# Where the selected and the window keys of the requests are transposed: TensorE and PSUM, or VectorE in 32 by 32 blocks

## The reference, cut to what matters

```python
def sample_layer(...):
    past_nsa = gather_pages(c_nsa, page_table)              # [k_cmp, v_cmp, k_slc, v_slc] rows
    kc, vc, cpos, ks, vs, ov = nsa_prepare(concat([past_nsa, nkv[:, :, :4]]), W)
    win_all = concat([win, nkv[:, :, 4:]])
    o_n = nsa_block(nq, qpos, ng, kc, vc, cpos, ks, vs, ov, win_all[:, :, 0], win_all[:, :, 1], wpos, tb)
def nsa_block(...):
    ls = einsum('bthgd,bhtnsd->bhgtns', q, kg) * scale + bias_s     # selected keys
    lw = einsum('bthgd,bshd->bhgts', q, kw) * scale + bias          # window keys
```

## Time and profile before

| | us |
|---|---|
| median of 3 runs | 2698.3 (2696.34 to 2704.59) |
| the profiled execution | 2699.43 |
| its span in the trace | 2697.6 |
| the stage of the requests in it | 807.3 to about 1082.9 |
| TensorE busy over the span | 2592.7 (96%) |

### The profile page before, as it was taken

The page is one execution under the profiler, slowest core; times in us unless marked ns, Lnnn a source line. Parts: engine busy times, 40 slices in busy tenths (PEclk is TensorE's granted clock), DMA queues, the critical chain, the costliest instruction groups (busy, mean ns, idle before and its releaser), DMA issues.

```text
span 2697.6 us, 29317 instructions
## 1 busy us (share of the span) xinstructions
PE 2592.7 (96%) x10863; PEld 1446.0 (54%) x10863; DVE 710.3 (26%) x1959; ACT 532.0 (20%) x1329; POOL 357.5 (13%) x568
## 2 busy tenths in 40 slices
PE   8999998988987999999999999999999999999999
PEld 4554665555555666566665455555555554444443
DVE  0010236665652344101012222222222220101222
ACT  0001025655652333000001121111011110010110
POOL 0000014444443000100001410000000000021110
PEclk9999999998998999999999999999999999999999
DMA  5324530030029776411023101111111115332300
GB/s 177 91 72 116 203 118 1 1 116 1 1 67 240 226 222 207 117 24 47 23 86 66 59 28 37 41 31 31 47 31 31 42 65 189 101 101 102 146 32 31
DMA packets 198599, 227.15 MB, mean 84 GB/s; under 512 B 52191, under 2 KB 149951, under 8 KB 196935
## 3 DMA queue, kind: packets, MB, share of 16 engines
q1 hardware_dynamic: 191674, 199.80, 25.0%
q0 software_dynamic: 5648, 16.33, 1.7%
q10 hardware_dynamic: 1168, 9.58, 1.1%
HBM read 203.60 MB, written 37.99 MB: 90 GB/s over the span
## 4 chain that ended last, share of the span: by engine, by line
PE 60%; ACT 0%; DVE 0%; issue 0%; DVEq 0%
PE ps L2071 24%; PE ps L2121 11%; PE ps L2024 9%; PE ps L2167 5%; PE ps L2017 4%; PE ps L2044 4%; PE ps L2125 1%; PE ps L2006 1%; PE ps L2170 0%; PE ps L2048 0%; PE ps L2078 0%; ACT arena L2257 0%; PE ps L2056 0%; PE ps L2151 0%; DVE arena L2379 0%; DVE qfT L2396 0%
## 5 line engine op out<-in xcount | busy, mean ns | idle before, releaser
L2071 PE MATMUL ps<-xT,qT 128*128 128x480 f32 (+1 forms) x2112 | 648.1, 469 | 0.0
L2071 PEld LDWEIGHTS ps<-xT,qT 128*128 128x128 f32 x2112 | 344.5, 191 | 296.4 <-issue 296.4
L2121 PE MATMUL ps<-arena 128*128 128x512 f32 x704 | 305.3, 593 | 0.0
L2024 PE MATMUL ps<-xT,arena 128*128 128x363 f32 (+1 forms) x768 | 238.1, 467 | 0.0
L2121 PEld LDWEIGHTS ps<-arena 128*128 128x128 f32 x704 | 132.6, 190 | 167.2 <-issue 166.9
L235 PE MATMUL ps<-arena,xT 128*128 128x512 f32 (+1 forms) x512 | 201.6, 552 | 2.9 <-DVE arena L324 1.5
L2024 PEld LDWEIGHTS ps<-xT,arena 128*128 128x128 f32 x768 | 145.4, 189 | 88.8
L929 ACT ACTIVATE arena<-arena 128x640 f32<-128x640 f32 (+15 forms) x256 | 162.8, 638 | 102.2 <-DVE arena L884 57.7
L795 PE MATMUL ps<-ident,arena 128*128 128x128 f32 (+4 forms) x880 | 148.6, 297 | 24.5 <-ACT xT L938 16.0
L983 POOL TENSOR_SCALAR arena<-arena,gates 128x55 f32<-128x55 f32 (+15 forms) x192 | 123.0, 650 | 324.8 <-DVE arena L892 324.6
L2341 DVE TENSOR_SCALAR qfT<-qfT 128x480 f32<-128x480 f32 (+1 forms) x88 | 35.1, 420 | 445.1 <-ACT qfT L2216 445.1
(11 more groups left out here) (299 smaller groups left out, 2465.0 us busy)
## 6 DMA issues: line engine op xcount, KB each, us to landing
arena<-in_w_ffn_down SPq DMA_DIRECT2D x66, 512.0 KB, 3.6
arena<-in_cache_fox_kv SPq DMA_DIRECT2D x72, 256.0 KB, 5.9
xT<-in_cache_fox_kv SPq DMA_DIRECT2D x56, 256.0 KB, 6.7
arena<-in_cache_nsa_kv SPq DMA_DIRECT2D x64, 192.0 KB, 4.7
qT<-in_w_ffn_up SPq DMA_DIRECT2D x22, 512.0 KB, 4.0
qT<-in_w_ffn_gate SPq DMA_DIRECT2D x22, 512.0 KB, 5.3
bias_rows<-rev_dram ACTq DMA_DIRECT2D x8, 1160.0 KB, 19.3
arena<-in_w_in SPq DMA_DIRECT2D x16, 512.0 KB, 5.4
```

What stands on the lines that cost most here:

```text
L2024: mm = pe.matmul(ps[:, 4 * (j % 2) + side, 0:n], at.w_gate[e][:, side, c, :], x[:, c, t0:t0 + n], start=(c == 0), stop=(c == KD - 1))
L2071: mm = pe.matmul(ps[:, 2 * (j % 3) + side, 0:n], at.w_ug[e][:, side, c, :], x[:, c, t0:t0 + n], start=(c == 0), stop=(c == KD - 1))
L2121: mm = pe.matmul(ps[:, q + h, :], hT[:, c, t0:t0 + m], at.w_down[:, load % RING, cols], start=(c == 0), stop=(c == NFF - 1))
```

## The change

The selected and the window keys no longer pass through TensorE and the ring. VectorE transposes them from SBUF to SBUF: one instruction takes a strip of 32 partitions and writes it, block by block of 32 by 32, to 32 other partitions. `selected_turned(r)` has 16 such instructions of 256 elements per partition, `window_turned(r)` 16 of 128, so a round has 32 and 32. They stand behind the copy of `p_fox1` and ahead of `forget_outcome`. `slc_turns`, `win_turns`, six ring entries and their six copies (three on ScalarE, three on VectorE) go. `slc_scores`, `win_scores` and SyncE's `raw_rows` now wait for VectorE's semaphores `slc_turned` and `win_turned`.

```diff
@@ ring_entries @@
-            yield from ((n, f"slc{x}{'ab'[r]}", r) for x in range(2) for r in range(2))
...
-            yield n, "wina", 0
-            yield n, "winb", 1
@@ SyncE @@
             def raw_rows(n):
-                sp.wait_ge(ring_filled, ring.index[n - 1, "slc1b"] + 1)
+                sp.wait_ge(slc_turned, 2 * n)
@@ TensorE @@
-            def slc_turns(n):
-                for x in range(2):
-                    for r in range(2):
-                        b = enter(n, f"slc{x}{'ab'[r]}")
-                        for j in range(4):
-                            mm = turn(b, j * P, P, at.raw[:, r, 2 * x + j // 2, j % 2, 256:384])
-                        mm.then_inc(ring_filled, 1)
-
-            def win_turns(n):
-                pe.wait_ge(win_in, 32 * (n + 1))
-                for r in range(2):
-                    b = enter(n, f"win{'ab'[r]}")
-                    for j in range(4):
-                        mm = turn(b, j * P, P, at.win[:, r, j, 0:P])
-                    mm.then_inc(ring_filled, 1)
...
             def slc_scores(n):
                 if n:
                     pe.wait_ge(nsa_saved, n)
+                pe.wait_ge(slc_turned, 2 * n + 2)
                 for x in range(2):
-                    consumed(n, f"slc{x}a")
-                    consumed(n, f"slc{x}b")
...
             def win_scores(n):
-                consumed(n, "wina")
-                consumed(n, "winb")
+                pe.wait_ge(win_turned, 2 * n + 2)
@@ ScalarE @@
-                    for x in range(2):
-                        save(n, f"slc{x}a", ...)
...
-                    save(n, "wina", at.winT[:, 0, :], ps[:, ring.bank(n, "wina"), :])
@@ VectorE @@
+            def selected_turned(r):
+                for q in range(4):
+                    for z in range(4):
+                        rows = at.raw[z * 32:(z + 1) * 32, r, :, :, 256 + q * 32:256 + (q + 1) * 32]
+                        columns = at.slcT[q * 32:(q + 1) * 32, r, :].rearrange("p (a q t) -> p a t q", a=4, t=2)
+                        ins = nc.vector.transpose(columns[:, :, :, z * 32:(z + 1) * 32], rows)
+                ins.then_inc(slc_turned, 1)
+
+            def window_turned(r):
+                for q in range(4):
+                    for z in range(4):
+                        ins = nc.vector.transpose(at.winT[q * 32:(q + 1) * 32, r, :].rearrange("p (j t) -> p j t", j=4)[:, :, z * 32:(z + 1) * 32],
+                                                  at.win[z * 32:(z + 1) * 32, r, :, q * 32:(q + 1) * 32])
+                ins.then_inc(win_turned, 1)
...
-                    for x in range(2):
-                        save(n, f"slc{x}b", ...)
                     dve.wait_ge(fox_exp, n + 1)
                     inverse(n, fox_inv, at.sums[:, FOX_C:FOX_C + 1], fox_inverse, 2 * n)
                     save(n, "p_fox1", at.pT_fox[:, 4:8, :], tiles(ring.bank(n, "p_fox1"), 4))
+                    dve.wait_ge(raw_in, 256 * (n + 1))
+                    for r in range(2):
+                        selected_turned(r)
+                    dve.wait_ge(win_in, 32 * (n + 1))
+                    for r in range(2):
+                        window_turned(r)
                     if n < N_ - 1:
                         forget_outcome(n)
...
-                    save(n, "winb", at.winT[:, 1, :], ps[:, ring.bank(n, "winb"), :])
```

More of the change, by code:

```diff
@@ L1228, in request_attention @@
      win_exp, imp_ready, imp_saved, pick_step, picked, slc_biased, nsa_coef, nsa_pv, nsa_step, nsa_saved, queries_ready,
-     neg_c_ready, set_ready) = k.sems(
+     neg_c_ready, set_ready, slc_turned, win_turned) = k.sems(
         "ring_filled", "ring_act", "ring_dve", "fox_scored", "fox_logits", "fox_exp",
@@ L1232, in request_attention @@
         "cmp_logits", "cmp_exp", "cmp_inverse", "win_exp", "imp_ready", "imp_saved", "pick_step",
-        "picked", "slc_biased", "nsa_coef", "nsa_pv", "nsa_step", "out_nsa_saved", "queries_ready", "neg_c_ready", "set_ready")
+        "picked", "slc_biased", "nsa_coef", "nsa_pv", "nsa_step", "out_nsa_saved", "queries_ready", "neg_c_ready", "set_ready",
+        "slc_turned", "win_turned")
     used = (ring_act, ring_dve)
@@ L1631, in _ @@
                 if now:
-                    slc_turns(n)
                     pe.wait_ge(fox_exp, n + 1)
@@ L1644, in _ @@
                     compressed(n)
-                    win_turns(n)
                     slc_scores(n)
@@ L1709, in _ @@
                     raw_rows(n, 1, 1)
-                    for x in range(2):
-                        save(n, f"slc{x}a", at.slcT[:, 0, x * 512:(x + 1) * 512].rearrange("p (a q t) -> p a t q", a=2, t=2),
-                             ps[:, ring.bank(n, f"slc{x}a"), :].rearrange("p (a t q) -> p a t q", a=2, t=2))
                     save(n, "p_fox0", at.pT_fox[:, 0:4, :], tiles(ring.bank(n, "p_fox0"), 4))
@@ L1852, in _ @@
                 if now:
-                    for x in range(2):
-                        save(n, f"slc{x}b", at.slcT[:, 1, x * 512:(x + 1) * 512].rearrange("p (a q t) -> p a t q", a=2, t=2),
-                             ps[:, ring.bank(n, f"slc{x}b"), :].rearrange("p (a t q) -> p a t q", a=2, t=2))
                     dve.wait_ge(fox_exp, n + 1)
```

## The result

The changed kernel takes 2708.28 us (median of 20 runs, 2702.89 to 2716.28) and the kernel before 2697.99 (20 runs, 2692.99 to 2708.72): a ratio of 1.0029 with an interval of 1.0020 to 1.0038. It is **slower by 0.3 to 0.4%**, where -2 us was forecast (2696.1). The time lies in the range, but the sign is wrong.

What follows compares the result with a forecast made beforehand. Copies were taken to bound the transposes, transfers the stretch from `fox_values` to the late pages, with idle VectorE as cover. Terms -7.2 + 0 + 5.0 = -2.2 us took the median from 2698.3 to 2696.1 us; range 2687 to 2716.

Steps and rivals of the forecast that it cites:

- The stretch of the transposes, 4 x 1.8: Ahead of `p_fox1`: without the selected-key copies it starts 1.8 us earlier in each of four rounds, -7.2 us.
- it holds in full: Behind `p_fox1`: all 7.2 us count, since SyncE's `values` and later transfers count from `fox_values` and move with it.
- The window keys, 1.0 lost to waits in the early rounds: TensorE drops eight transposes, 1.03 us a round; in the first three rounds it waits that much longer for keys, counted 0.
- The price of a transpose: On VectorE: 0.43 us for 256 elements per partition and 0.30 for 128, taken from copies of like size.
- X: VectorE's time for the 64 transposes of one round, forecast as 23.4 us; above about 25.6 the whole change loses.
- the cheap end: VectorE's transposes overlap by 0.08 us, X = 17.8 us a round, kernel at 2690.5 us; chance 0.15.
- The cover of the early rounds: First three rounds: VectorE's 24.85 us of work fits the 24.7 us before the first small score, cost 0.
- The last round, +5.0: Before the last small scores: 24.2 us of VectorE work against 19.21 us of cover, so they come 5.0 us later.
- SyncE's new wait: At `raw_rows`, now waiting for VectorE 13.8 us after `p_fox1`: SyncE's queue arrives later, 17.4 us behind, so it costs nothing.
- The sum: Whole kernel: -7.2 + 0 + 5.0 = -2.2 us, median from 2698.3 to 2696.1 us.
- half the rate: Rival: VectorE transposes at half rate, X = 35.8, `small_scores` waits for compressed copies, +39.0 us, 2737; chance 0.12.
- A cost on top of each transpose: Rival: each VectorE transpose costs some 0.1 us more to fill and drain, X = 29.8, +14.7 us, 2713; chance 0.13.

Runs made afterwards that it cites:

- e8: Kernel before, but VectorE transposes the selected keys from the second round on; window keys stay on TensorE: ratio 0.9999 to the kernel before.
- e11: Same switches as e8, timed again: selected keys on VectorE from the second round on, against the kernel before: ratio 0.9993, median 2699.36 us.
- e2: Kernel before, but VectorE transposes the selected keys in all rounds; window keys stay on TensorE: ratio 1.0011 to the kernel before, median 2703.00 us.
- e6: Same switches as e2, timed again: selected keys alone on VectorE in all rounds, against the kernel before: ratio 0.9998.
- e12: Same switches as e2, a third time: selected keys alone on VectorE in all rounds, against the kernel before: ratio 1.0006, median 2704.79 us.
- e3: Kernel before, but VectorE transposes the window keys in all rounds; selected keys stay on TensorE: ratio 1.0010 to the kernel before.
- e10: Changed kernel, but in the last round one request's window keys (16 of 32 transposes) go through TensorE again: ratio 0.9999 to the kernel before.
- e7: The changed kernel built and timed again, against the kernel before: ratio 1.0041.
- e9: Kernel before, but VectorE transposes selected and window keys in the last round only: ratio 1.0038 to the kernel before, 6 runs.
- e5: The kernel before, written through the variants' switches with nothing changed, against the kernel before: ratio 0.9998.
- e15: The kernel before through the switches, nothing changed, timed again against the kernel before: ratio 0.9989.

## Why the prediction was wrong, point by point

- **What bounds the kernel:** right. The copies set the pace among the transposes, the transfers from `fox_values` to the late pages, and VectorE's idle time is the cover.
- **The stretch of the transposes, 4 x 1.8:** the mechanism was right, and the size was right where nothing took it back. Against the three traces of before, the second, third and last rounds are 1.4, 2.1 and 1.7 us shorter in e8 and e11, 1.6, 0.0 and 1.3 in e2, e6 and e12 (the clock took back the third of e6 and e12), and 1.7, 0.9 and 1.2 in the changed kernel, where a gap of 1.15 us ahead of the small scores takes some of it. **The first step that failed is "it holds in full".** In the first round the values come out of a DMA queue that was filled long before, and do not move with `fox_values`: the four rounds together kept 4.2 us in the changed kernel, not 7.2. I had shown only for the second round that SyncE waits for TensorE, and carried it over to the first. There `hidden` starts 47.8 to 52.9 us after the stage's start, whatever the kernel.
- **The window keys, 1.0 lost to waits in the early rounds:** right (e3).
- **The price of a transpose:** 0.451 and 0.317 from start to start instead of 0.43 and 0.30, X = 24.6 instead of 23.4. The copies were the right neighbours and the cheap end was wrong, since nothing overlaps. The estimate from the page "VectorE: DVE Perf Modes" of the Trainium skill, section "The three transpose paths", 0.44 and 0.31, was nearer: its 311 ns against 303 here.
- **The cover of the early rounds:** right within the price. TensorE waits 1.15 us ahead of the small scores in two of three rounds, about what the window transposes took. The waits for FoX keys behind it are not shorter but 0.7 to 0.9 us longer (3.1, 2.9 and 2.6 us a round on the means of the two traces, 2.3, 2.0 and 1.9 in the three of before). So the transfers take some of the 1.8 us in these rounds too.
- **The last round, +5.0:** it measured +6.0, by X alone (25.1 less 5.08 for half the window, e10). **The second step that failed is its price: what was left out is the clock**, 1.6 to 2.2 us more in the finishing pass behind a gap of 7 us (21.4, 21.5 and 21.9 us against 19.8). I priced the wait as if TensorE came back from it at full speed. The trace of before shows otherwise in its first round, where eight transposes take 1.94 us behind a gap, and 1.09 in the earlier trace rows:

```profile
825.42 1.94 PE L1406 MATMUL ps<-ident,arena 128*128 128x128 f32 x8 [6.31 <-DVE arena L1730]
```

- **SyncE's new wait:** right, it never showed. `raw_rows` start right behind `selected_values`.
- **The sum:** by the means of the traces (279.6 us against 276.0) the stage is 3.6 us longer, and it was forecast 2.2 shorter. Of these 5.8, 1.0 is X in the last round, 1.9 the clock behind it, 1.4 the first round, and 1.5 the parts of 1.8 that the later ones did not keep. With the trunk the kernel is 2.7 us longer in the traces. The ratios say 8 and 11 us, the medians 10 and 11. The part of this beyond the traces goes with the lower granted clock of the runs (0.9831 and 0.9843, before 0.9864); its cause stays open.
- **The rivals:** none was it. The one on the slow side, half the rate, had the right place, the compressed copies behind the transposes, and its condition, that the sum turns at X = 25.6, was close. X was 24.6, at which the forecast's own sum is -1.0; the clock and the savings that were not kept did the rest. A cost on top of each transpose was there, but about 0.02 us and not 0.1.

## What to carry to other kernels

Work that moves to an engine with idle time must fit into its idle stretch in every round. Here the last round was the one to measure, since the work that covers it there is shorter. Price the wait that would come out of it together with the clock: a gap of 7 us on TensorE was followed by products at half speed, one of 1.2 us was not. Look for such a gap in the timeline that you have; the kernel before had one of 6.31 us with slow transposes behind it. An argument about who waits for whom, read in one round, holds for the first and the last only after their rows have been read as well.

## What the runs showed of the hardware

- A 32 by 32 block transpose of fp32 from SBUF to SBUF on VectorE takes 437 ns for 256 elements per partition and 303 ns for 128, 0.451 and 0.317 us from start to start on changing partitions. That is a copy of the same size and 11 or 12 ns more, also with only 32 partitions in use.
- TensorE's granted clock was 0.50 after gaps of 6.97 and 6.98 us and stayed full after one of 1.16 us. Four records of 512 columns took 1.92 instead of 1.03 us.
- Half speed that a gap brings can take the place of half speed further on: the trunk took 1613.1 us behind the gaps of e7 and e9, and 1614.8 in before. In the first trace of the changed kernel it took 1614.6, so this is not so each time.
- The same kernel spans 2695.8 or 2703.4 us in two traces (e5 and e15), and the 8 us lie ahead of the stage, where the granted clock is 0.97 and 0.96. So a difference of 0.1% cannot be read from one trace each, and a trace read by stage shows where it is not.
